# Thirty-two more prompt tokens on gathered experts in a hybrid decoder step; dense expert phases over 416 columns

## The reference

```python
def block(xb):
    q = (xb @ w_q).astype(jnp.float32).reshape(PEER_BLOCK, PEER_HEADS, 2, PEER_QDIM // 2)
    s = jnp.einsum('bhpd,hpkd->bhpk', q, sub_keys.astype(jnp.float32))
    sv, si = lax.top_k(s, PEER_TOPK)
    cand = (sv[:, :, 0, :, None] + sv[:, :, 1, None, :]).reshape(PEER_BLOCK, PEER_HEADS, PEER_TOPK * PEER_TOPK)
    cv, ci = lax.top_k(cand, PEER_TOPK)
    ...
    idx = i1 * N_KEYS + i2
    gate = jax.nn.softmax(cv, axis=-1)
    act = jax.nn.gelu(jnp.einsum('bhkd,bd->bhk', u_emb[idx], xb).astype(jnp.float32), approximate=False)
    return jnp.einsum('bhk,bhkd->bd', (gate * act).astype(v_emb.dtype), v_emb[idx])
```

## Time and profile before

| | |
|---|---|
| time, median of 3 runs | 2151.61 us (2148.58 to 2164.17) |
| span of the profiled execution | 2149.9 us |
| PE busy | 2046.7 us (95%) |
| PE weight loads busy | 1800.8 us (84%) |
| DVE busy | 1532.6 us (71%) |
| ACT busy | 757.6 us (35%) |
| POOL busy | 609.0 us (28%) |
| moved by DMA | 437.47 MB, mean 203 GB/s |
| granted TensorE clock, mean | 0.976 |

### The profile page before, as it was taken

The page is one execution under the profiler, slowest core; times in us unless marked ns, Lnnn a source line. Parts: engine busy times, 40 slices in busy tenths (PEclk is TensorE's granted clock), DMA queues, the critical chain, the costliest instruction groups (busy, mean ns, idle before and its releaser), DMA issues.

```text
span 2149.9 us, 35762 instructions
## 1 busy us (share of the span) xinstructions
PE 2046.7 (95%) x14513; PEld 1800.8 (84%) x14513; DVE 1532.6 (71%) x2662; ACT 757.6 (35%) x940; POOL 609.0 (28%) x515
## 2 busy tenths in 40 slices
PE   7999987788999998999999999999999999999997
PEld 7997866667447788998889889989999999999997
DVE  6526564776237899788898898897767666776676
ACT  5324443443021023345444544554322222222223
POOL 8144537450000000122332241212333233322330
PEclk9999988989999999999999999999999999999999
DMA  5112210011141214677887797779998888888873
GB/s 191 60 53 61 61 38 2 8 42 52 51 152 40 76 53 157 224 265 267 296 327 258 264 360 274 249 287 358 396 342 301 310 324 305 304 307 318 318 267 124
DMA packets 175772, 437.47 MB, mean 203 GB/s; under 512 B 12192, under 2 KB 92832, under 8 KB 165280
## 3 DMA queue, kind: packets, MB, share of 16 engines
q1 hardware_dynamic: 127552, 242.81, 32.5%
q0 software_dynamic: 36864, 134.23, 16.8%
q10 hardware_dynamic: 11232, 58.73, 6.7%
HBM read 368.57 MB, written 67.17 MB: 203 GB/s over the span
## 4 chain that ended last, share of the span: by engine, by line
PE 71%; DVE 10%; ACT 2%; issue 2%; POOL 2%; DMA 2%; ACTq 0%; DVEq 0%; POOLq 0%
PE bank L1923 29%; PE bank L1837 21%; PE bank L1742 3%; PE bank L1846 3%; PE bank L1820 3%; PE bank L1821 3%; DVE u_lo L2474 2%; DMA sca<-in_pu_rows,pick 2%; PE bank L1807 1%; DVE sca L2480 1%; PE bank L1787 1%; PE bank L1468 1%; PE bank L1379 1%; DVE isel L2609 1%; DVE hot_a L2532 1%
## 5 line engine op out<-in xcount | busy, mean ns | idle before, releaser
L1837 PE MATMUL bank<-xhi,u_hi 128*128 128x448 f32 x1008 | 379.6, 377 | 6.2 <-DVE u_lo L2474 6.2
L761 POOL DMA_INDIRECT sca<-in_pu_rows,pick x128 | 173.1, 1352 | 721.0 <-DVE sdot L2480 441.3
L1923 PE MATMUL bank<-w_hi,v_hi 128*128 128x448 f32 x1024 | 374.3, 365 | 0.6 <-ACT actb L1149 0.6
L1923 PE MATMUL bank<-w_lo,v_hi 128*128 128x448 f32 x1024 | 374.0, 365 | 0.0
L1923 PE MATMUL bank<-w_hi,v_lo 128*128 128x448 f32 x1024 | 374.0, 365 | 0.0
L1837 PE MATMUL bank<-xhi,u_lo 128*128 128x448 f32 x1008 | 369.4, 366 | 0.0
L1837 PE MATMUL bank<-xlo,u_hi 128*128 128x448 f32 x1008 | 368.6, 366 | 0.0
L761 POOL DMA_INDIRECT rows_v<-in_pv,pick x128 | 195.0, 1523 | 424.2 <-DVE xs L2689 373.5
L1202 ACT ACTIVATE v_hi<-v_raw 128x4096 fp32r<-128x4096 f32 x32 | 116.1, 3628 | 424.4 <-PE bank L1923 398.6
L2713 DVE TENSOR_TENSOR v_lo<-v_raw,v_hi 128x4096 fp32r<-128x4096 f32 x32 | 141.6, 4424 | 163.7 <-ACT v_hi L1202 163.7
L1837 PEld LDWEIGHTS bank<-xhi,u_hi 128*128 128x128 f32 x1008 | 189.6, 188 | 20.2 <-issue 6.5
(11 more groups left out here) (640 smaller groups left out, 3511.3 us busy)
## 6 DMA issues: line engine op xcount, KB each, us to landing
u_raw<-in_pu SPq DMA_DIRECT2D x64, 1024.0 KB
v_raw<-in_pv SPq DMA_DIRECT2D x32, 2048.0 KB, 16.9
act_scratch<-actb ACTq DMA_DIRECT2D x64, 448.0 KB
gate_scratch<-gst ACTq DMA_DIRECT2D x14, 2048.0 KB
wts<-act_scratch SPq DMA_DIRECT2D x32, 896.0 KB
gring<-gate_scratch SPq DMA_DIRECT2D x32, 896.0 KB
wring<-in_w_q SPq DMA_DIRECT2D x4, 2048.0 KB, 8.7
wp_raw<-in_w_in SPq DMA_DIRECT2D x7, 1024.0 KB, 6.6
```

The source lines that it names most:

```text
L761: pool.indirect_dma_start(dst, None, rows[:, :], bass.IndirectOffsetOnAxis(pick[:, s:s + 1], 0)).then_inc(s_row[s % RING], 16)
L1837: ins = mm(bank[b][:, 0:DS], lhsT, rhs[:, 0:DS], **on)
L1923: ins = mm(bank[c][:, 0:DS], lhsT, rhs[q][:, e, :], **on)
```

## The change

The first 32 prompt tokens (`XT`) leave the dense tokens, which are now 416 (`DS`): tokens 32 to 447, the slice `DENSE` of the transposed activations. The tiles for keys and gates are cut anew: tile 0 has 64 tokens, of which the first 32 get no quads, the tiles 1 to 3 have 128, 128 and 128. There are 104 quads in place of 112.

The 32 tokens are gathered like the last tile, but each has four copies, on partitions 0, 32, 64 and 96 onwards, and each copy has a quarter of the token's 128 picks. So 32 more gathers and 32 more dot products on DVE serve them, and 32 more gathers and adds in the value stage, into a sum of their own (`few_sum`). Eight small matmuls with the selecting matrix `few_sel` (`few_columns`) add the four copies up and put the result into columns 416 to 447 of the value banks, before the last two groups. The picks and gates of the 32 tokens are copied to the four places by eight small DMAs on ACT's queue at group 12; their rows are dotted from the 41st position on (`S_FIRST`) and come first among the adds. Their normalized activations are copied by four DMAs on SP's queue.

The lists that spread quads and dots over the groups are new: the four tiles have 12, 13, 13 and 11 groups. In tile 0 every third group has two quads and two dots, the others no quads and four dots; in the tiles 1 and 2 a group has mostly two quads and three dots; in tile 3, two quads and four dots or four quads and three dots. The ungated groups have 4 and 3 dots in place of 3 and 2. Two of the tile loops on PE, which were hardware loops, are written out. In the value stage a group has five adds, two before and three after the splits. The last tile's residual and output are moved in two pieces.

```diff
+XT = 32
+XQ = 128 // XT
+DS = SEQ - 64 - XT
+FTILES = [(0, 64), (64, 128), (192, 128), (320, 128), (SEQ - 64, 128)]
+DENSE = slice(XT, XT + DS)
+DX = DS + XT
+LTILES = [(0, 128), (128, 128), (256, 128), (384, 64), (DX, 128)]
...
-GROUPS_OF = [0, 16, 16, 13, 4]
+GROUPS_OF = [0, 12, 13, 13, 11]
...
-QUADS = [2] * 32 + [4 if j in (2, 6, 12) else 2 for j in range(13)] + [4] * 4
+QUADS = [2 * (j % 3 == 0) for j in range(12)] + [4 if j in (2, 6, 10) else 2 for j in range(13)] * 2 + [2 + 2 * (j % 2) for j in range(11)]
...
-HEAD_DOTS, TAIL_DOTS = 6, [3, 2]
-DOTS = [5 if j in (13, 29) else 4 if j % 16 > 11 else 2 for j in range(32)] + [1 if q == 4 else 2 for q in QUADS[32:45]] + [3] * 4
+HEAD_DOTS, TAIL_DOTS = 6, [4, 3]
+DOTS = [2 if q else 4 for q in QUADS[0:12]] + [4 if j == 12 else 1 if QUADS[12 + j] == 4 else 3 for j in range(13)] * 2 + [4 if q == 2 else 3 for q in QUADS[38:49]]
...
+PAIRS = SLOTS + XT
+S_FIRST = 40
+DOT_ORDER = [("s", i) for i in range(S_FIRST)] + [("e", i) for i in range(XT)] + [("s", i) for i in range(S_FIRST, SLOTS)]
+ADD_ORDER = [("e", i) for i in range(XT)] + [("s", i) for i in range(SLOTS)]
...
+            sp.wait_ge(S("xf_ready"), 1)
+            for c in range(XQ):
+                sp.dma_start(few_x[XT * c:XT * c + XT, :], xf_rows(0)[0:XT, :]).then_inc(s_copy, 16)
...
-            for s in range(SLOTS):
-                gather(s, rows_u[s % RING], pu_rows, "row_used")
...
+            for s, which in enumerate(DOT_ORDER):
+                if s == S_FIRST:
+                    pool.wait_ge(s_copy, FEW_PICKS)
+                gather(s, which, rows_u[s % RING], pu_rows, "row_used")
...
+            act.wait_ge(s_copy, FEW_ROWS)
...
+                if g == HEAD0:
+                    act.wait_ge(S("picked"), 2)
+                    for c in range(XQ):
+                        rs, cs = slice(XT * c, XT * c + XT), slice(XT * c, XT * c + XT)
+                        act.dma_start(few_pick[rs, :], pick0[0:XT, cs]).then_inc(s_copy, 16)
+                        act.dma_start(few_gate[rs, :], gate[0:XT, 0, cs]).then_inc(s_copy, 16)
...
-                    xh, xl = xhi[:, kt, :], xlo[:, kt, :]
+                    xh, xl = xhi[:, kt, :], xlo[:, kt, DENSE]
...
+            def few_columns():
+
+                pe.wait_ge(S("row_added"), XT)
+                for c in range(KD):
+                    mm(bank[c][:, DS:DX], few_sum[:, 128 * c:128 * c + 128], few_sel, start=False, stop=False,
+                       skip_group_check=True)
...
+                for g in range(G0[pos], G0[pos] + GROUPS_OF[pos]):
+                    j = g - HEAD0
+                    quads = range(QUAD0[j], QUAD0[j + 1])
+                    for quad in quads[0:2]:
+                        quad_rows(quad)
+                    split_u(g + 1)
+                    for quad in quads[2:]:
+                        quad_rows(quad)
+                    for r in range(DOT0[j], DOT0[j + 1]):
+                        sample_dot(r)
+                    if pos < 4:
+                        between(pos, g - G0[pos])
...
+            link(STT(out=cabf[0:XT, 0, :], in0=isel[0:XT, 0, :], scalar=128.0, in1=isel[0:XT, 1, :], op0=ALU.mult, op1=ALU.add))
+            dve.tensor_copy(pick0[0:XT, :], cabf[0:XT, 0, :]).then_inc(S("picked"), 1)
...
+                adds = PAIRS // EG
+                for r in range(adds):
+                    if r == (adds // 2 if g else 0) and g + 1 < EG:
                         split_v(g + 1)
                         split_weights(g + 1)
-                    sample_add(4 * g + r)
+                    sample_add(adds * g + r)
...
-                sp.dma_start(y_o[t0:t0 + n, :], x1_late[t][0:n, :]).then_inc(s_out, 16)
+                for r0, t0, n in PIECES[t]:
+                    sp.dma_start(y_o[t0:t0 + n, :], x1_late[t][r0:r0 + n, :]).then_inc(s_out, 16)
```

More of the change, by code:

```diff
@@ L22 @@
 TILES = [(t * 128, 128) for t in range(PT)] + [(SEQ, SAMP)]
-DS = SEQ - 64
-FTILES = [(0, 128), (128, 128), (256, 128), (384, 64), (DS, 128)]
+XT = 32
[5 more added lines that the diff above has]
+LTILES = [(0, 128), (128, 128), (256, 128), (384, 64), (DX, 128)]
+PIECES = [[(0, XT + 128 * t, 128)] for t in range(3)] + [[(0, XT + 384, DS - 384)] * (DS > 384) + [(DS - 384, 0, XT)], [(0, DX, 128)]]
+NPIECES = sum(len(p) for p in PIECES)
 MCH = 128
@@ L254, in hybrid_step @@
         xhi = sb("xhi", [128, KD, DS], f32r, scope=first)
-        sb("gap0", [128, KD * 64], scope=first)
+        sb("gap0", [128, KD * (512 - DS)], scope=first)
         sub_sc = ExitStack()
@@ L298, in hybrid_step @@
         mx8 = sb("mx8", [128, 2, HEADS], scope=first)
+        few_x = sb("few_x", [128, D], scope=first)
+        pick0 = sb("pick0", [128, SLOTS], u32, scope=first)
         first.close()
@@ L1211, in _ @@
                 if g + 2 == UG:
+                    act.wait_ge(S("row_used"), E_DOTTED)
                     high_values(0, 0)
@@ L1250, in half_out @@
                 own(S("yrms_ready"))
-            for t, (t0, n) in enumerate(FTILES[0:4]):
+            for t, (t0, n) in enumerate(LTILES[0:4]):
                 act.wait_ge(S("x2_ready"), t + 6)
@@ L1851, in _ @@
             pe.wait_ge(S("u_hi_ready"), 1)
-            for m, (u, x) in enumerate(((u_hi, xhi), (u_hi, xlo), (u_lo, xhi))):
+            x_low2 = xlo[:, :, DENSE]
+            for m, (u, x) in enumerate(((u_hi, xhi), (u_hi, x_low2), (u_lo, xhi))):
                 if m == 1:
@@ L1880, in _ @@
                 ins.then_inc(S("hk_done"), 1)
[L1882 to L1895 removed]
+                for g in range(G0[pos], G0[pos] + GROUPS_OF[pos]):
+                    first_q, last_q = QUAD0[g - HEAD0], QUAD0[g - HEAD0 + 1]
+                    half = (last_q - first_q) // 2
+                    for e in range(GU):
+                        dots(0, 8, g, e)
+                        for quad in range(first_q + half * e, first_q + half * e + half):
+                            gate_quad(quad)
             for g in range(GATED_END, UG):
@@ L1939, in _ @@
                     sums(i, 2 + q)
+            few_columns()
             sums(0, EG - 2)
@@ L2477, in sample_dot @@
             def sample_dot(s):
+                kind, i = DOT_ORDER[s]
+                if s == S_FIRST:
+                    dve.wait_ge(s_copy, FEW_ROWS)
+                row, dot = (xs, sdot[:, i:i + 1]) if kind == "s" else (few_x, few_dot[:, i:i + 1])
                 dve.wait_ge(s_row[s % RING], 16 * (s // RING + 1))
-                dve.tensor_tensor_reduce(rows_u[s % RING], rows_u[s % RING], xs[:, :], 1.0, 0.0, ALU.mult, ALU.add,
-                                         sdot[:, s:s + 1]).then_inc(S("row_used"), 1)
+                dve.tensor_tensor_reduce(rows_u[s % RING], rows_u[s % RING], row[:, :], 1.0, 0.0, ALU.mult, ALU.add, dot
+                                         ).then_inc(S("row_used"), 1)
             def between(pos, j):
@@ L2514, in one_hots, with quad_rows @@
                 link(TT(g2_, r, g1, ALU.subtract))
-                j = G0[pos] - HEAD0
-                for k in range(n // 4):
-                    quad = t0 // 4 + k
+                first_k, ahead = (XT // 4, 0) if t == 0 else (0, (t0 - XT) // 4)
+                if t == 0:
+                    link(dve.tensor_reduce(few_sel, ident[:, :].rearrange("p (c t) -> p t c", t=XT), AX.X, ALU.add))
+                def quad_rows(quad):
+                    k = quad - ahead + first_k
                     s = 2 * (quad % 4)
```

152 lines of the change are left out of this document (72 added, 80 removed).

## The result

The changed kernel takes **2173.6 us** (median of 4 runs, 2167.3 to 2184.9) against 2152.9 for the kernel before (4 runs beside it): 1.0099 of the time, 95% interval 1.0059 to 1.0139. It is slower by one per cent, where the prediction had 2088 us, three per cent faster, and a range that ended at 2112. Its profiled execution spans 2167.8 us.

A forecast was written before the change was run, and what follows sets the result against it. TensorE was taken to bound the value stage, with DVE nearly full beside it in the gated stage. Terms -43.6 + 1.5 + 1 - 0.7 - 22.5 + 0 + 0.6 = -63.7 us gave a 2086.2 span, 2088 us; range 2072 to 2112.

The forecast's parts named there:

- The columns' worth: Dense matmuls: 32 columns fewer save 14.2 ns each, bounds 13.9 and 14.6; 43.6 us over the value stage's 3072.
- Gated stage: Gated dot groups: 546.5 us for 569.0 before, 22.5 less, where TensorE alone would give 44.7.
- the lining up: Gated groups: waits found by lining up TensorE, ACT and DVE group by group, each row back after 7 us.
- The rival: Dot stage and value opening: rows back in 9 to 10 us, not 7; 2108 us, chance 0.20.
- late gathered rows must exceed the slack before they cost anything: Value stage: v_lo and w_lo take 6.3 of 18.1 us, so about 8 us of lateness per group costs nothing.
- this rival: Value stage: rows late by over 8 us in every group hold v_lo; gain gone, 2131 us, chance 0.04.
- Ungated groups: Three ungated dot groups: 30.2 us, no gain, bounds 27.4 and 35; two dots more and more rows to wait for.
- Opening of the value stage: Start of the value stage: slack used up by shorter groups, fifth add and its row; 1 us more, bounds 0 and 5.
- few_columns: Value stage: eight small plain-f32 matmuls added, 1.5 us more, bounds 0.8 and 2.3.
- tail: End of the kernel: last tile stored by two transfers, 0.6 us more, bounds 0 and 1.3.
- The slower rival: Dot stage: ring of four row buffers decides from a 15.5 us round trip; 2213 us at 17.1 throughout, chance 0.04.
- wrong signs: Gated stage: TensorE never idle, or DVE waiting over 40 us for rows; value group over 18.3 us, v_lo waited for.

The follow-up runs named there:

- five buffers: Changed kernel with five row buffers instead of four for the value stage's adds, dots keeping four: 2127.8 us, 0.987 of the kernel before.
- the moved add: Changed kernel with each value group's first add between v_lo and w_lo instead of behind both, four buffers: 2128.6 us, 0.988 of the kernel before.
- the columns alone: Changed kernel without the 32 tokens' gathers, dots and adds, 416 columns kept, dots dealt anew: 2090.1 us, 0.972 of the kernel before.
- all the vector work and no extra rows: Changed kernel doing all 160 dots and adds, but 32 of each on a fixed buffer without a gather: 2092.7 us, 0.975 of the kernel before.
- seven and five buffers: Changed kernel with seven row buffers for the dots (the last 13 keep four) and five for the adds: 2091.5 us, 0.971 of the kernel before.

## Why the prediction was wrong, step by step

- **The columns' worth: right.** 14.2 ns forecast for 32 columns. In the value stage 202.7 (19.46 / 96) less 188.9 (18.13 / 96) is 13.8; in the dot stage 204.4 (9.81 / 48) less 188.9 (9.066 / 48) is 15.5; the mean, 14.7, lies at the upper bound of 14.6. By the Trainium skill (TensorE: Matmul & The Clock Gate, Back-to-back issue gap) it would be 13.3, an estimate from its warm gap. The value stage alone is as near to that as to 14.2, the dot stage isn't; and since 448 columns took 202.7 ns in one run and 206.7 in another, half a nanosecond can't be told here.
- **Gated stage: the sum right, its assumption not.** 546.5 was forecast, 542 to 545 measured in each kernel whose rows came in time, and the tiles within 2 us. (The "28 dots more" of its summary are 30, 147 for 117; the sums by tile have the right numbers.) In the changed kernel it was 580.8. The step that failed is the lining up with "each row back 7 us after its slot is freed". Gathers stand in line on POOL, and the row shown above took 12.1 us from its gather and 14.5 from the release of its buffer. The rival named this, but priced it as 2 or 3 us more a row and so 5 to 15 us in all: a mean applied to what bites in bunches. In tile 0 every third group took 13.3 to 19.8 us for some 11, and in tile 3 single ones 13.9 to 19.8 for 12.
- **What late rows do to TensorE: a term was missing.** In the changed kernel, from group 12 to the value stage, each of the six stops of 4.53 to 9.77 us was followed by matmuls 347 ns apart, for 1.3 to 3.7 us. There 56 matmuls ran so, at 158 ns more each 8.8 us; in the kernel before none did in that stretch. The Trainium skill says this (TensorE: Matmul & The Clock Gate, "HAM oscillation"): a kernel that waits between short stretches of matmuls begins each anew at the low clock. The trace agrees for these six. The prediction has no term for it.
- **Value stage: the step that failed is "late gathered rows must exceed the slack before they cost anything".** That holds for a row whose request doesn't depend on the work it delays. With five adds and four buffers, the add ahead of the splits uses the buffer that the first add behind them frees. Its lateness comes back each group. The slack of 8 us only puts the cost off: at 1.5 us a group it is used up in five to six groups (an estimate from 19.6 and 18.1), and the first seven groups did take 18.1 us. In the end DVE was so far behind that the last group paid 10 us more. What counts is the loop's own length, and all its terms were in the rows: two adds 2.59, v_lo 4.42, w_lo a fourteenth under 2.02 make 8.9, so a row that comes back later than 9.2 us after its release, in group after group, sets the period, and the earlier trace rows had one of 17.1. The prediction gave this rival 0.04, on a condition ("late by over 8 us in every group") that isn't its condition. The kernel before had four adds for four buffers: there each buffer comes round once a period, and a row has 19.5 us less one add. With the loop open the stage took 586 to 587 us (five buffers, or the moved add), where the sum had 584.5: the terms were right, and what bounds the stage was not.
- **Ungated groups: direction foreseen, size not.** 30.2 us with bounds of 27.4 and 35; 39.9 measured, and 37 to 39 in the variants that keep the order. Even the columns alone have 33.9, and 38.4 with all the vector work and no extra rows. The failed term is the row: the four dots ahead of the last u_lo had their rows asked for one behind another, as the dots of the last gated group freed the buffers; the last was there 21.0 us after its gather, where the earlier trace rows had 17.1 (chain of the changed kernel):

```profile
1488.65 21.03 DMA sca<-in_pu_rows,pick
```

- **Opening of the value stage, few_columns and tail: right.** The first seven groups took 18.1 to 18.2 us; the group with few_columns takes 1.7 us more where TensorE sets the pace, and 1.5 was forecast; the tail 12.7 against 13.5. The end of the value stage was not: see its last group.
- **The slower rival** (a ring of four sets the dot stage) had the right mechanism and the wrong place and threshold: it was worked out for a mean round trip over the whole stage, 15.5 us. For two groups of four dots in a row, 9.1 us each, the threshold is 9.1 less one dot.
- **What the prediction said would show it:** of its wrong signs one came and one nearly. Value groups took over 18.3 us, though with w_lo waited for and not v_lo. DVE waited 32.8 us for rows in the gated groups, where the sign was 40, and 48.4 in all with the head and the ungated groups; 33 us of such waits already cost 36 us of the stage.

The three misses add to 89.5 us. By stage, seven and five buffers give back 38.2 + 3.0 + 43.6 = 84.8 of them.

## What to carry to other kernels

Before adding one more user to a ring of buffers, write down the loop of each slot: from its release through the request, the transfer and all that stands ahead of its next use, to the next release. If that loop fits into a period with as many buffers as uses per period, one use more can put the longest stretch of other work into it. Slack elsewhere then only puts the cost off by some periods; here one buffer, or one instruction moved out of the loop, took it away. Count the uses where they are densest and not in the mean: dealt evenly, the dots of tile 0 needed no further buffer. In this kernel a stage where no engine was full and the transfers were below their best rate was the sign of it.

## What the runs showed of the hardware

- **The clock after a stop.** In the changed kernel the stops of 4.53 to 9.77 us were all followed by matmuls at the lower clock; of shorter ones some were (2.07, 2.60 us), others not (2.67, 1.62). In the changed kernel's ungated stage the mean granted clock was 0.87.
- **A gather's record grows beside DVE.** Alone its issue took 0.94 us; begun beside an add of 1.29 us 1.93; beside w_lo (1.89) 2.34; and beside v_lo, 4.42 us with two operands in SBUF, 4.88. Each time it ended 0.8 to 0.9 us after DVE's instruction did, as if its own 0.94 us began only then. From the value stages of the changed kernel and of the one with the moved add:

```profile
1782.94 4.88 POOL L786 DMA_INDIRECT rows_v<-in_pv,pick  x1 [5.44 <-DVE xs L2747]
1790.28 1.93 POOL L786 DMA_INDIRECT rows_v<-in_pv,pick  x1 [2.45 <-DVE xs L2747]
```
```profile
1782.31 2.34 POOL L786 DMA_INDIRECT rows_v<-in_pv,pick  x1 [7.11 <-DVE xs L2747]
```

  The Trainium skill (GPSIMD Engine Reference, Specifications) says that GpSimd shares its way into SBUF with VectorE, and that DVE's instructions with two SBUF inputs contend with it. The rows agree. Nothing here tells how much of a row's 10.7 us this makes; the gather in the loop was the 1.93 one.
- **The same matmul, two paces.** In the value stage 448 columns took 202.7 ns in one run and 206.7 in another; 416 columns took 188.9 ns in every profiled run that TensorE set the pace of, but 187.8 in one; each time at a granted clock of 1.00. So a matmul's time can differ by 0.6 to 2% between runs, as much as this change moved.
